# Weight transfers split by partitions instead of by k-tiles in a hybrid decoder step

## The reference, cut to what matters

```
xn = rmsnorm(x);  z = xn @ w_in            # 2048 x 10320: q, k, v, index columns, conv input, gates
q, k = rmsnorm per head;  an indexer scores keys, top-k keys per query, softmax, values
a = attention @ w_attn_br                  # 1024 x 2048
c = silu(layernorm(causal depthwise conv, width 31)) @ w_conv_br      # 1024 x 2048
h = x + (sigmoid(ga) * a + sigmoid(gb) * c) @ w_out                   # 2048 x 2048
y = h + (silu(rmsnorm(h) @ w_gate) * (rmsnorm(h) @ w_up)) @ w_down    # 2048 x 5632, 5632 x 2048
```

## Time and profile before

| | |
|---|---|
| profiled execution | 2124.8 us, of which the span from first to last instruction is 2123.3 us |
| TensorE matmuls | 2049.6 us busy (97%) |
| TensorE weight loads | 1948.1 us (92%) |
| VectorE | 1248.0 us (59%) |
| ScalarE | 891.5 us (42%) |
| GpSimd | 166.4 us (8%) |
| mean granted TensorE clock | 0.977 of full speed |
| SP's DMA queue | 518480 packets, 263.55 MB, 46.0% of 16 engines' span |
| GpSimd's DMA queue | 25824 packets, 84.55 MB, 12.2% |

### The profile page before, as it was taken

One profiled execution on the slowest core, in us unless ns is written; L12 is line 12 of the kernel. 1 busy time (PEld: TensorE's weight loads), 2 busy tenths in 40 slices (PEclk: granted clock), 3 DMA queues, 4 the chain that ended last, 5 costly groups with the idle time before them and its releaser, 6 DMA issues.

```text
span 2123.3 us, 40316 instructions
## 1 busy us (share of the span) xinstructions
PE 2049.6 (97%) x14517; PEld 1948.1 (92%) x14517; DVE 1248.0 (59%) x2293; ACT 891.5 (42%) x1640; POOL 166.4 (8%) x293
## 2 busy tenths in 40 slices
PE   6989998989998999999999999999999999999997
PEld 5956998989996778999999999999999999999997
DVE  5325987646666999875755555544455554455553
ACT  6423443434334333346444554443344443344443
POOL 6300000021112220010000000000000000000012
PEclk9997999999997999999999999999999999999999
DMA  9362543377774997565755555555555555555573
GB/s 242 86 117 71 135 123 86 105 257 233 239 239 156 331 323 215 140 158 140 208 141 157 141 156 143 153 147 150 151 146 157 141 157 142 155 148 149 153 204 108
DMA packets 545492, 350.54 MB, mean 165 GB/s; under 512 B 15122, under 2 KB 524346, under 8 KB 545007
## 3 DMA queue, kind: packets, MB, share of 16 engines
q1 hardware_dynamic: 518480, 263.55, 46.0%
q0 software_dynamic: 25824, 84.55, 12.2%
q10 hardware_dynamic: 1088, 1.05, 0.2%
HBM read 338.91 MB, written 10.83 MB: 165 GB/s over the span
## 4 chain that ended last, share of the span: by engine, by line
PE 68%; DVE 1%; ACT 0%; issue 0%; POOL 0%; POOLq 0%; DVEq 0%; ACTq 0%
PE psG L1398 21%; PE psG L1399 21%; PE psG L1400 21%; PE psS L1395 2%; PE psM L1400 1%; PE psM L1399 1%; PE psM L1398 1%; PE psM L1392 0%; PE psG L1392 0%; DVE stat L1204 0%; PE psT L1392 0%; DVE OL L1267 0%; ACT L L774 0%; PE psS L1392 0%; DVE L L1199 0%
## 5 line engine op out<-in xcount | busy, mean ns | idle before, releaser
L938 DVE TENSOR_TENSOR WL<-RAW,WH 128x512 fp32r<-128x512 f32 (+1 forms) x996 | 674.8, 692 | 639.4 <-ACT WH L554 637.3
L554 ACT ACTIVATE WH<-RAW 128x512 fp32r<-128x512 f32 (+1 forms) x996 | 614.7, 628 | 843.0 <-PE psG L1400 792.0
L1398 PE MATMUL psG<-XH,WH 128*128 128x320 f32 (+1 forms) x2688 | 857.1, 319 | 15.8 <-issue 7.6
L1399 PE MATMUL psG<-XL,WH 128*128 128x320 f32 (+1 forms) x2688 | 842.5, 313 | 0.0
L1400 PE MATMUL psG<-XH,WL 128*128 128x320 f32 (+1 forms) x2688 | 840.8, 313 | 0.0
L1398 PEld LDWEIGHTS psG<-XH,WH 128*128 128x128 f32 x2688 | 510.9, 190 | 48.3 <-issue 39.4
L1399 PEld LDWEIGHTS psG<-XL,WH 128*128 128x128 f32 x2688 | 511.3, 190 | 1.4
L1400 PEld LDWEIGHTS psG<-XH,WL 128*128 128x128 f32 x2688 | 511.2, 190 | 0.0
L1398 PE MATMUL psG<-MH,WH 128*128 128x320 f32 x960 | 297.0, 309 | 0.4 <-DVE ML L1367 0.4
L1400 PE MATMUL psG<-MH,WL 128*128 128x320 f32 x960 | 295.7, 308 | 0.0
L1399 PE MATMUL psG<-ML,WH 128*128 128x320 f32 x960 | 295.2, 307 | 0.0
(11 more groups left out here) (348 smaller groups left out, 1676.2 us busy)
## 6 DMA issues: line engine op xcount, KB each, us to landing
RAW<-in_w_in SPq DMA_DIRECT2D x160, 512.0 KB, 5.2
RAW<-in_w_ffn_down SPq DMA_DIRECT2D x96, 512.0 KB, 4.9
RAW<-in_w_ffn_gate SPq DMA_DIRECT2D x88, 512.0 KB, 4.9
RAW<-in_w_ffn_up SPq DMA_DIRECT2D x88, 512.0 KB, 4.6
kst<-in_cache_k POOLq DMA_DIRECT2D x64, 512.0 KB, 4.2
vst<-in_cache_v POOLq DMA_DIRECT2D x64, 512.0 KB, 6.1
RAW<-in_w_out SPq DMA_DIRECT2D x32, 512.0 KB, 4.7
RAW<-in_w_attn_br SPq DMA_DIRECT2D x16, 512.0 KB, 5.0
```

What stands on the lines that cost most here:

```text
L554: act.activation(WH[:, s % 2, 4 * r:4 * r + 4, c], RAW[:, s, 4 * r:4 * r + 4, c], ACT.Copy).then_inc(hi_done, 1)
L938: dve.tensor_tensor(WL[:, s, k, c], RAW[:, s, k, c], WH[:, s % 2, k, c].bitcast(F32), ALU.subtract).then_inc(lo_done, 1)
L1398: pe.matmul(out, WH[:, s % 2, k], hi, start=start, stop=False)
L1399: pe.matmul(out, WH[:, s % 2, k], lo, start=False, stop=False)
```

## The change

In `columns`, a unit of 16 k-tiles is loaded as partitions 0 to 63 with all its k-tiles and then partitions 64 to 127, instead of k-tiles 0 to 7 and then 8 to 15 on all partitions. A transfer still has 1024 rows of 512 bytes. The semaphore and what waits for it stay, and so do the pairs of `halves`, of ikiw and of 12 k-tiles.

```diff
             def columns(G_, s, w, col, k0=0, m=KT, first=False):
                 c = bass.ds(col if isinstance(col, int) else sp.snap(col), P)
-                load(G_, s, RAW[:, s, 0:8, :], w[:, k0:k0 + 8, c], RAW[:, s, 8:KT, :], w[:, k0 + m - 8:k0 + m, c], first)
+                if m == KT:
+                    half = P // 2
+                    load(G_, s, RAW[0:half, s], w[0:half, k0:k0 + m, c], RAW[half:P, s], w[half:P, k0:k0 + m, c], first)
+                else:
+                    load(G_, s, RAW[:, s, 0:8, :], w[:, k0:k0 + 8, c], RAW[:, s, 8:KT, :], w[:, k0 + m - 8:k0 + m, c], first)
```

## The result

The changed kernel takes 2146.84 us (median of four runs, 2141.69 to 2149.62) against 2124.44 us before: a ratio of 1.0111 with a 95% interval of 1.0092 to 1.0131. It is 22.4 us slower; forecast were 2125.3 us and a range of 2117 to 2134 us. The time is that of the first rival.

A forecast was written before the change was run, and what follows sets the result against it. From 900 to 2000 us it took matmuls on TensorE to set the end. Only the exposed qk place added time, +1.4 us, all else 0: 2125.3 us on the median, range 2117 to 2134 us.

The forecast's parts named there:

- the first rival: The ga stage becomes DMA-bound: 16 pairs cost 16 x 1.4 = 22 us, giving 2146 us; chance 0.10.
- What bounds the kernel, and 900 to 2000 us: From 900 to 2000 us matmuls set the end; weights have 3.1 us of spare in the FFN, cost 0.
- The rate on 64 partitions: Weight transfers run at x_sample's 228 GB/s: the first lands 0.7 us later, the pair 1.4 us later.
- The exposed place at 115 to 124 us: At the first qk unit, a straight chain from landing to TensorE puts the whole 1.4 us onto the path.
- The first loads, "Cost 0": Four pairs issued before 30 us: 5.6 us of lateness fits just inside 6 us of spare, cost 0.
- the third rival: Faster, at most 7.2 us from shorter waits (2116.7 us), more only from a clock shift; faster by over 0.5%: 0.04.
- The ga stage, "Cost 0 in the sum": At 676 to 835 us ScalarE is late by about 1 us in a few units; TensorE's 9.7 us unit covers it.
- are not held up by the weights alone: Argument against the ga stage becoming DMA-bound: value pages fill the other partitions meanwhile; no size of its own.
- the cover of a unit: In ga TensorE still has the unit between, 9.7 us, when ScalarE gets a weight late.
- The rivals of no effect: 512-byte rows keep the engines too slow to reach the limit; landings stay 4.1 and 5.2 us, 2123.9 us; chance 0.21.
- a faster kernel: New pairs quicker: at most 7.2 us gained from ScalarE and cache-page waits, 2116.7 us; faster by over 0.5%: 0.04.

The follow-up runs named there:

- e1: The changed kernel with the 20 pairs of ga and gbA put back to k-tiles: 2124.11 us, ratio 1.0007 to the kernel before.
- e4: The changed kernel's adjacent halves as destinations, but reading from HBM the rows of the kernel before (outputs wrong): 2143.23 us, ratio 1.0092.
- e3: The changed kernel, but split into even and odd partitions instead of lower and upper halves: 2124.56 us, ratio 1.0009.
- e5: The changed kernel with 56 of the 64 value pages loading only their first 512 columns (outputs not the reference's): 2123.63 us, ratio 0.9986.
- e9: The changed kernel with ScalarE's copy of osb moved ahead of the rounding that waits for weights in ga: 2147.11 us, ratio 1.0091.
- e10: The changed kernel run again, on the same chip as e9: 2145.04 us, ratio 1.0085.
- e2: The kernel before with the split by partitions only in the 20 pairs of ga and gbA: 2148.36 us, ratio 1.0114.
- e6: The kernel before with 56 of the 64 value pages loading only their first 512 columns (outputs not the reference's): 2124.81 us, ratio 0.999.
- e7: The kernel before with one 1 MB transfer on all 128 partitions per full pair instead of two: 2127.19 us, ratio 1.0003.
- e8: The kernel before with the 16 pairs issued during ga split into halves, issued by SP and ScalarE at nearly the same time: 2128.34 us, ratio 1.0007.

## Why the prediction was wrong

- **What bounds the kernel, and 900 to 2000 us:** right. The slower pairs cost nothing there, as e1 shows with 196 of them in place.
- **The rate on 64 partitions:** right in kind and near in size. The pair lands 6.8 us after line 355's issue, predicted 6.6; the first transfer 5.1, predicted 4.8; the FFN's DMA share is 0.73, predicted 0.8. e4 shows that it is the destination, as was read from x_sample's rows; e3 adds that it is not the number of partitions, since every second one of them costs nothing.
- **The exposed place at 115 to 124 us:** right in the trace. ScalarE's wait is 4.61 us against 2.78 and TensorE's 7.00 us against 5.18, so +1.8 us for a predicted +1.4:

```profile
127.37 2.19 ACT L558 ACTIVATE WH<-RAW 128x512 fp32r<-128x512 f32 x4 [4.61 <-DMA RAW<-in_w_in]
...
130.32 0.65 PE L1402 MATMUL psG<-XH,WH 128*128 128x336 f32 x1 [7.00 <-ACT iwT L636]
```

  Whether it reaches the end can't be said: e1 has it (TensorE waits 6.9 us there), and its interval of 0.9989 to 1.0025 holds both 0 and 1.8 us.
- **The first loads, "Cost 0":** wrong in the trace. The prediction looked at the reads of the weights alone. But the store of xT_scratch, from another queue, runs beside these pairs; it lands 14.5 us after its issue, 10.3 before, VectorE waits for it (first before, then after), and ScalarE, about to round the third unit, for VectorE (11.29 us, 6.83 before):

```profile
DVE iqs L974 <- DMA xT_scratch<-xTs: 3.9, 1, 3.9
...
DVE iqs L978 <- DMA xT_scratch<-xTs: 8.3, 1, 8.3
```

  Together with the 1.8 us above, the first qk matmul starts 6.6 us later (130.32 against 123.76). It starts at 128.2 to 131.7 us in e1, e4, e5, e9 and e10, which load these pairs in adjacent halves too, and at 123.6 to 125.4 us in e2, e3, e6, e7 and e8. That the stage ga begins 2.5 us early all the same is no merit of that step. It goes with a clock shift of the kind that the third rival names: from 130 to 200 us the granted clock is 0.84 before and 0.94 after, as the busy tables show.

```profile
130.00:200.00 70.00, 66.94 (x236) 37.46 (x236) 21.64 (x48) 15.32 (x42) 2.90 (x4) 0.84 0.30 45
...
130.00:200.00 70.00, 66.60 (x263) 38.47 (x264) 26.56 (x58) 20.01 (x52) 4.78 (x7) 0.94 0.49 75
```

  In the profile of e10 it is 0.84 there, and ScalarE's read that stood at 689.24 us before comes 6.5 us late, at 695.75. Whether the higher clock follows from the late start stays open; the medians of e1 and e5, which have the late start too, are no longer than those without it.
- **The ga stage, "Cost 0 in the sum":** this step failed. It treated the 1.4 us as a latency, to be set against a spare of 2.4 us and a cover of 9.7 us, one pair at a time. But the rows at hand said that the engines were 0.99 busy: with nothing free, lateness is handed on from pair to pair, and ScalarE's waits grew to 16.8 us, past the cover. The right comparison was engine time asked for per unit against TensorE's 9.7 us: a share of 0.99 is 9.6 us before, and 1.4 us more make 11.0 us, 1.3 us too much in each of 16 units. The stage lost 27 us.
- **The size:** more went into it than the step counted. The value packets slow down with the weights (161 to 194 ns), which the sentence that the engines "are not held up by the weights alone" denied; this adds 1.0 us per unit. And the cover of a unit was smaller than claimed, since ScalarE has osb behind the rounding; by e9 this mattered little. SP is held up as well: its issues, 0.44 us long in this stage before, take up to 9.95 us, as in this piece of its order of time:

```profile
759.19 9.95 SPq L354 DMA_DIRECT2D RAW<-in_w_in  x1
769.32 5.95 SPq L355 DMA_DIRECT2D RAW<-in_w_in  x1
```

- **The rivals:** the first one happened, at the place and with TensorE waiting between 690 and 835 us, though not for WL or WH, as named, but for osb (in e9 for WL too). Its price of 22 us came close to the 22.4 measured, but by luck: the stage lost 27 us in place of 16 x 1.4, and some of that is won back elsewhere. The trace gave it far more than the chance of 0.10: a share of 0.99, VectorE nearly full and 0.3 us of spare in one pair all stood in its favour, and of what stood against it, the sentence on the value pages had no row behind it. The rivals of no effect and of a faster kernel fall: narrow packets of 512 bytes do slow down, by 39% (29.7 to 41.2 ns).

## What to carry to other kernels

Where DMA engines are busy all the time, compare the engine time that a step of the loop asks for, all queues together, with the time of the engine that sets the pace; a spare of a few microseconds per transfer does not protect when every transfer is late. The first comes from a view that groups packets by queue, share times stretch over a whole stage; it is good to about a tenth, since shares can pass 1. And when a transfer is cut by partitions, let every piece spread over the whole of SBUF, as the even and odd partitions do: its bytes and its rows are then the same to the engines as before.

## What the runs showed of the hardware

The cost of an adjacent half depends on what is written beside it: 512-byte packets took 29.7 ns on all partitions, 29.3 ns on every second one (e3: 0.382 x 1280 / 16675), 41 ns on one half, and 33.8 ns when both halves were under way from two queues. The slower packets also slow another queue's, from 161 to 194 ns, though that queue writes to all partitions. TensorE, which now waits up to 13.8 us at a time, is granted a clock of 0.89 in 715 to 795 us after the change, 1.00 before, so some matmuls ran at the lower of the two levels, 1.2 GHz; whether this lengthened a stage that waits for its transfers, no run shows.
